# Two mixture-of-experts stages: an earlier weight load on the SP queue, and filler matmuls moved on TensorE

## The chip, the cores and the metric

One core of a Trainium2 chip runs the whole program. The metric is device time in microseconds (us). Before the change it is 985.3 us, the median of three runs (984.91 to 985.96).

## The reference, cut to what matters

The program is one inference step of a two-layer diffusion backbone for 128 context tokens and 256 latent tokens (384 rows of width 1024). Each layer is a mixer followed by a mixture of experts; the change touches only the start of the two mixtures:

```
h = modulate(x, norm2_g, shift, scale)                     # 384 x 1024
p_group, logits_e = softmax(h @ w_group + b), h @ w_expert + b
expert_id, weight = top-1 group, top-2 experts within it   # 768 (token, expert) pairs over 16 experts
hid = silu(h @ w1[e]) * (h @ w3[e])                        # EXPERT_DIM = 256
y   = sum over the two experts of weight * (hid @ w2[e])
x   = x + gate * y
```

## The kernel before, in words

Everything is written out by hand: one program per engine, ordered by semaphores. The mixture stands twice, as `experts(0)` after the attention and recurrence layer and as `experts(1)` after the convolution layer. The 768 pairs are laid into 14 positions of 128 slots (`POSITIONS`); a position serves one or two experts, each with an "up" block (w1 and w3, 2 MB) and a "down" block (w2, 1 MB). The blocks rotate through rings of five buffers (`ring`, `dring`), so the first five up blocks (positions 0, 0, 1, 1, 2) find their buffers empty and the later ones wait for a position to be used.

A mixture begins in this order. The router (VectorE, with small products on TensorE) gives each pair its slot. TensorE turns the normed rows h token-wise (L2139, `h_turned`). ScalarE copies the turned rows out of PSUM (L894, `htok_ready`, six copies) and stores them to `h_rows` in device memory with three DMAs on its own queue (L896, `h_stored`). VectorE builds six comparison columns (L1447, `owners_ready`), TensorE multiplies them (L2145, `owners_T`), and VectorE makes indices of the product (`rows_ready`). GpSimd then waits for `h_stored` and `rows_ready` and picks the rows of positions 0, 1 and 2 from `h_rows` by indirect DMA (L584). TensorE turns the picked rows (`fill`, L2119), ScalarE copies them (`slots`, L882), and the loop over positions begins with `up(0)` (L2094).

Beside that path TensorE has other work before `up(0)`, all in program order: in layer 0 two pairs of products with the last adaLN weights (`ada(2, 6)`, L1694, of which the second pair follows the owners product and needs ScalarE's copy L684 of the pair before), the second owners product with the pairs' weights (L2156, after VectorE's `weights_ready`), and the turned gates (L2158). ScalarE copies the gates (L911), stores them (L915, 4 KB), waits for that store, reads them back broadcast (L918), and only then copies the picked rows of position 0 (L882). `keep(n)` (L1709) issues n matmuls of 128x256 whose result nobody reads; in the trace each is two instructions.

The SP queue carries the weights. Its program is in order too: `static` loads (L445) that wait until a buffer of the adaLN weights is free, `expert_up` (L469) and `expert_down` (L484). In layer 0 the blocks (0,0), (0,1), (1,0) of the down ring lie in buffers of the adaLN weights and wait for `ada_used` 38, the end of the second `ada(2, 6)`; the block (1,1) lies in the buffer of h and waits for `h_turned` and `h_stored`, in both layers; (2,0) has a buffer that is free when the projection before is done.

Of the kernel before, what the change touches and what calls it, by code (L numbers as in the profile page):

```python
# [28 lines left out]
NB = TOK // P  # L29
# [243 lines left out]
def build(nc, A):  # L273
    with ExitStack() as ctx:
        sems = {}

        def S(name):

            if name not in sems:
                sems[name] = ctx.enter_context(nc.semaphore(name))  # L280
            return sems[name]

        def ge(eng, name, v):

            if isinstance(v, int) and v <= 0:
                return
            eng.wait_ge(S(name), v)
# [6 lines left out]
        def bank(b, n=512, o=0):  # L294
            return ps[:, b * 512 + o:b * 512 + o + n]
# [146 lines left out]
        @block.sync  # L442
        def _(sp):
            def load(n, dst, src):
                sp.dma_start(dst, src).then_inc(S(f"raw_full{n % RAW}"), 16)  # L445

            def fetch(n):

                if n < FIRST:
                    sp.dma_start(ada_first(n), A["weights"][n]).then_inc(S(f"ada_full{n}"), 16)  # L450
                else:
                    load(n, raw[:, n % RAW, :], A["weights"][n])

            def static(a, b):
                for n in range(a, b):
                    if n >= FIRST + RAW:
                        name, v = FREED[n - RAW]
                        sp.wait_ge(S(name), v)
                    if B_P1 <= n < B_P1 + RAW:
                        sp.wait_ge(S("down_used"), POSITIONS - 2 if n == B_P1 else POSITIONS)  # L460
                    fetch(n)

            def expert_up(l, q, z):

                m = BLOCK_AT[q, z]
                if m >= RING:
                    sp.wait_ge(S("up_used"), POSITIONS * l + BLOCKS[m - RING][0] + 1)
                e = P * (EXPERTS * l + BLOCKS[m][2])
                sp.dma_start(ring(m).rearrange("p k n -> p (k n)"), A["experts_up"][e:e + P, :]).then_inc(S(f"up_full{m % RING}"), 16)  # L469

            def expert_down(l, q, z):

                m = BLOCK_AT[q, z]
                if m >= RING:
                    sp.wait_ge(S("down_used"), POSITIONS * l + BLOCKS[m - RING][0] + 1)
                elif m == RAW:
                    sp.wait_ge(S("h_turned"), 6 * (l + 1))
                    sp.wait_ge(S("h_stored"), 16 * NB * (l + 1))
                elif l == 0 and m < RAW:
                    sp.wait_ge(S("ada_used"), N_ADA0)  # L480
                else:
                    sp.wait_ge(S("lo_done"), (U_PW1, U_END)[l])
                e = P * (EXPERTS * l + BLOCKS[m][2])
                sp.dma_start(dring(m).rearrange("p k n -> p (k n)"), A["experts_down"][e:e + P, :])\  # L484
                    .then_inc(S(f"down_full{m % RING}"), 16)

            def expert_loads(l):

                for q in range(2):
                    for z in range(2):  # L490
                        expert_up(l, q, z)
                if l == 0:
                    static(B_P1 - 6, B_P1)
                sp.wait_ge(S("unit_used"), (U_PW1, U_END)[l])
                if l == 0:
                    sp.wait_ge(S("h_stored"), 16 * NB)
                    sp.wait_ge(S("picked0"), 16)
                    for q, z in ((0, 0), (0, 1), (1, 0), (1, 1)):
                        expert_down(l, q, z)
                    expert_up(l, 2, 0)  # L500
                    expert_down(l, 2, 0)
                else:
                    expert_up(l, 2, 0)
                    for q, z in ((2, 0), (0, 0), (0, 1), (1, 0), (1, 1)):
                        expert_down(l, q, z)
                expert_up(l, 3, 0)
                for q in range(4, POSITIONS):
                    expert_up(l, q, 0)
                    expert_down(l, q - 1, 0)
                expert_down(l, POSITIONS - 1, 0)  # L510
                if l == 0:
                    static(B_P1, B_P1 + 1)
                for z in range(2):
                    sp.wait_ge(S(f"rows_stored{z}"), 16 * (POSITIONS // 2) * (l + 1))
                for b in range(NB):
                    for c in range(2):
                        sp.dma_start(got[:, c, b, :], y_rows[TOK * c + P * b:TOK * c + P * b + P, :]).then_inc(S(f"got_rows{b}"), 16)
                if l == 0:
                    sp.wait_ge(S("up_used"), POSITIONS)
                    sp.dma_start(inverse, A["shape_constants"][:, T_I:T_I + I_W]).then_inc(S("in_inverse"), 16)  # L520

            static(0, B_P1 - 6)

            sp.wait_ge(S("oblo_ready"), 4)
            sp.wait_ge(S("oalo_ready"), NB)
            sp.wait_ge(S("pv_done"), len(PAIRS))
            expert_loads(0)
            static(B_P1 + 1, len(SLOTS))
            sp.wait_ge(S("cs_ready"), KC)
            expert_loads(1)  # L530

            for b in range(NB):
                sp.wait_ge(S("rows_added"), 2 * NB + b + 1)
                dst = A["out0"][0] if b == 0 else A["out1"][0, P * (b - 1):P * b, :]
                sp.dma_start(dst, got[:, 0, b, :]).then_inc(S("out_y"), 16)
            sp.wait_ge(S("out_kv"), 32)
            sp.wait_ge(S("out_state"), 64)
            sp.wait_ge(S("out_y"), 48)
# [1134 lines left out]
        def _(pe):  # L1673
# [25 lines left out]
            def keep(n, out=None, left=par[:, A_WR:A_WR + P], right=par[:, A_WR:A_WR + 256]):  # L1699

                if out is None:
                    i = slot[0] % 8
                    if i == 0:
                        ge(pe, "mod_ready", slot[0] // 8 + 1 if slot[0] else 0)
                    if i % 2 == 0:
                        pe.wait_ge(S("adarow_ready"), slot[0] // 2)
                    out = bank(7, 256, 256 * (i % 2))
                for _ in range(n):
                    mm(out, left, right, start=True, stop=True)  # L1709
# [348 lines left out]
            def experts(l):  # L2058
# [78 lines left out]
                for b in range(6):  # L2137
                    for k in range(4 * (b % 2), 4 * (b % 2) + 4):
                        last = nc.tensor.transpose(bank(b, P, P * (k % 4)), hfk[:, k, P * (b // 2):P * (b // 2) + P], ident)  # L2139
                    last.then_inc(S("h_turned"), 1)  # L2140
                if l:
                    keep(6, bank(6, 256))
                for i in range(6):
                    pe.wait_ge(S("owners_ready"), 6 * l + i + 1)
                    ins = mm(bank(7, POSITIONS, 64), column[:, i, :], named[:, i, :], start=(i == 0), stop=(i == 5))  # L2145
                ins.then_inc(S("owners_T"), 1)
                pe.wait_ge(S("htok_ready"), 2 * NB * (l + 1))
                if l == 0:
                    ada(2, 6)
                    pe.wait_ge(S("adarow_ready"), 19)  # L2150
# [103 lines left out]
            norm(1)  # L2254
            ada(2)
            experts(0)

# [81 lines left out]
            for j in range(2, 8):  # L2340
# [6 lines left out]
                elif j == 6:  # L2347
                    ada_columns(5)
            norm(3)
            experts(1)  # L2350

# [55 lines left out]
```

## Time and profile before

| | |
|---|---|
| median of three runs | 985.3 us |
| profiled execution: its time | 985.96 us |
| profiled execution: its span | 983.9 us |
| TensorE busy | 900.8 us, 92% of the span |
| VectorE, ScalarE, GpSimd busy | 406.7, 289.7, 263.1 us |
| chain that ended last | TensorE 75%, VectorE 9%, DMA 9%, ScalarE 4% |
| SP's DMA queue (q1) | 189.80 MB, 50.5% of 16 engines' span |

The span is the time of the instructions in the trace; the execution's own time also holds what lies around them. Busy times are averages over stages that differ much: the change is at 366 to 391 us in layer 0 and at 777 to 795 us in layer 1, and is read there.

### The profile page before, as it was taken

The page shows a single profiled execution, that of the slowest core. Times are in us where ns is not written, and L with a number is a line of the kernel's source. Part 1 is how long each engine was busy: PE and PEld are TensorE (multiplying, and loading weights), DVE is VectorE, ACT ScalarE, POOL GpSimd, SP SyncE. Part 2 cuts the span into 40 slices and gives each one's busy share as a digit, 9 for nine tenths or more (in the row PEclk, how much of TensorE's full clock was granted, in tenths as well). Part 3 has the DMA queues.
Part 4 walks back from the last instruction along what each step waited for, and adds up shares of the span by engine and source line. Part 5 has one row for each costly group of instructions (what it writes and reads, how often), then busy time and mean ns, then how long its engine had stood idle before and what let it go on. Part 6 is the DMA issues. An engine that isn't in the chain of part 4 may idle for free.

```text
span 983.9 us, 13906 instructions
## 1 busy us (share of the span) xinstructions
PE 900.8 (92%) x5729; PEld 578.3 (59%) x5729; DVE 406.7 (41%) x762; ACT 289.7 (29%) x537; POOL 263.1 (27%) x175
## 2 busy tenths in 40 slices
PE   3899999978797998998999989999999899989996
PEld 1688898755565985333333379888588743323332
DVE  1653665566635462222223463222625602222245
ACT  2632243332433243111111364121552521101112
POOL 0156353300003301233233306230360113333330
PEclk9999999998996997999999999999999889999998
DMA  9675335412424958999886543330449959999815
GB/s 379 261 257 214 129 135 204 149 44 89 171 91 145 419 177 322 403 378 401 299 313 230 186 163 129 129 130 1 174 179 417 364 187 377 403 362 380 294 64 202
DMA packets 41598, 230.08 MB, mean 234 GB/s; under 512 B 14112, under 2 KB 15168, under 8 KB 21824
## 3 DMA queue, kind: packets, MB, share of 16 engines
q1 hardware_dynamic: 22608, 189.80, 50.5%
q0 software_dynamic: 14528, 28.61, 8.1%
q10 hardware_dynamic: 4400, 10.77, 3.1%
q8 instruction: 46, 0.75, 0.3%
q14 instruction: 16, 0.13, 0.0%
HBM read 279.58 MB, written 19.81 MB: 304 GB/s over the span
## 4 chain that ended last, share of the span: by engine, by line
PE 75%; DVE 9%; DMA 9%; ACT 4%; issue 2%; POOL 1%; ACTq 0%; POOLq 0%; DVEq 0%
PE ps L2094 17%; PE ps L1723 8%; PE ps L2108 8%; PE ps L1725 8%; PE ps L1724 8%; PE ps L1694 4%; DMA Z<-experts_up,par 4%; PE ps L2119 2%; DMA att<-h_rows,par 2%; PE ps L1858 2%; DVE Z L1180 2%; DMA xT<-x_columns 1%; DVE Z L1059 1%; PE ps L1709 1%; PE ps L1715 1%
## 5 line engine op out<-in xcount | busy, mean ns | idle before, releaser
L547 POOL TENSOR_TENSOR wlo<-raw,whi 128x1024 fp32r<-128x1024 f32 x57 | 139.2, 2462 | 355.4 <-ACT whi L663 353.0
L2094 PE MATMUL ps<-Z,att 128*64 128x512 f32 x704 | 192.5, 605 | 6.3 <-DMA Z<-experts_up,par 6.3
L2094 PEld LDWEIGHTS ps<-Z,att 128*64 128x64 f32 x704 | 58.1, 139 | 100.6 <-issue 100.6
L1723 PE MATMUL ps<-hhi,whi 128*128 128x384 f32 x296 | 104.9, 354 | 6.7 <-DVE hlo L1295 3.0
L1724 PE MATMUL ps<-hlo,whi 128*128 128x384 f32 x296 | 101.0, 341 | 0.0
L1725 PE MATMUL ps<-hhi,wlo 128*128 128x384 f32 x296 | 100.9, 341 | 0.0
L1059 DVE TENSOR_TENSOR att<-att,ps 128x256 f32<-128x256 f32 x28 | 11.8, 421 | 190.4 <-ACT att L870 184.7
L663 ACT ACTIVATE whi<-raw 128x1024 fp32r<-128x1024 f32 x58 | 59.8, 1054 | 86.3 <-DMA raw<-weights 56.2
L2108 PE MATMUL ps<-raw,att 128*64 128x512 f32 x272 | 80.2, 598 | 0.0
L1723 PE MATMUL ps<-whi,hhi 128*128 128x256 f32 (+1 forms) x264 | 74.9, 284 | 2.4 <-DVE hlo L1570 1.7
L1724 PE MATMUL ps<-wlo,hhi 128*128 128x256 f32 (+1 forms) x264 | 73.7, 279 | 0.0
L1725 PE MATMUL ps<-whi,hlo 128*128 128x256 f32 (+1 forms) x264 | 73.5, 279 | 0.0
L2094 PE MATMUL ps<-spare,att 128*64 128x512 f32 x160 | 72.4, 595 | 0.0
L597 POOL DMA_INDIRECT y_rows<-att,par x28 | 34.2, 1222 | 138.7 <-DVE att L1507 137.1
L1507 DVE SCALAR_TENSOR_TENSOR att<-ps,par,slot_gate 128x512 f32<-128x512 f32 x52 | 39.0, 750 | 72.5 <-PE ps L2108 72.5
L1723 PEld LDWEIGHTS ps<-hhi,whi 128*128 128x128 f32 x296 | 56.9, 192 | 16.9 <-issue 8.7
L875 ACT ACTIVATE att<-ps 128x256 f32<-128x256 f32 x28 | 10.7, 384 | 169.6 <-PE ps L2076 169.5
L1724 PEld LDWEIGHTS ps<-hlo,whi 128*128 128x128 f32 x296 | 57.0, 193 | 0.0
L1725 PEld LDWEIGHTS ps<-hhi,wlo 128*128 128x128 f32 x296 | 56.7, 192 | 0.0
L1180 DVE COPY_PREDICATED Z<-con,ps 128x1024 f32<-128x1024 uint32 x24 | 31.0, 1311 | 53.6 <-PE ps L1858 36.5
L584 POOL DMA_INDIRECT att<-h_rows,par x28 | 28.3, 1011 | 89.6 <-DVE par L1463 42.2
L1723 PEld LDWEIGHTS ps<-whi,hhi 128*128 128x128 f32 x264 | 49.7, 188 | 4.3 <-issue 3.2
(332 smaller groups left out, 1487.0 us busy)
## 6 DMA issues: line engine op xcount, KB each, us to landing
raw<-weights SPq DMA_DIRECT2D x69, 1024.0 KB, 4.9
Z<-experts_up SPq DMA_DIRECT2D x26, 2048.0 KB, 10.8
raw<-experts_down SPq DMA_DIRECT2D x20, 1024.0 KB, 9.0
spare<-experts_up SPq DMA_DIRECT2D x6, 2048.0 KB, 12.1
Z<-weights SPq DMA_DIRECT2D x8, 1024.0 KB, 16.5
hf<-experts_down SPq DMA_DIRECT2D x6, 1024.0 KB, 9.1
spare<-experts_down SPq DMA_DIRECT2D x6, 1024.0 KB, 8.9
Z<-y_rows SPq DMA_DIRECT2D x12, 512.0 KB, 6.0
```

The costliest lines, as they stand in the source:

```text
L547: nc.gpsimd.tensor_tensor(unit_view(wlo, u), raw_unit(n, half), unit_view(whi, u).bitcast(F32), ALU.subtract)\
L584: pool.indirect_dma_start(picked[q % 3], None, h_rows[:, :], bass.IndirectOffsetOnAxis(ap=ri[:, OVERFLOW + ORDER[q]:OVERFLOW + ORDER[q] + ...
L597: pool.indirect_dma_start(y_rows[:, :], bass.IndirectOffsetOnAxis(ap=ri[:, o:o + 1], axis=0), rows, None, bounds_check=2 * TOK - 1, oob_is ...
L663: nc.scalar.activation(unit_view(whi, u), raw_unit(n, half), ACT.Copy)\
L1180: V.copy_predicated(AT[:, b, :, :], mask[:, l, :].unsqueeze(1).broadcast_to([P, HEADS, P]), bank(gram_bank(i), 1024).rearrange("p (n i) -> ...
L1507: V.scalar_tensor_tensor(out=dst[:, c], in0=bank(4 + d), scalar=slot_weight[:, n:n + 1], in1=slot_gate[:, c], op0=ALU.mult, op1=ALU.mult). ...
L1694: last = mm(ps[q:q + COLS, o:o + 256], scond[:, k, :], weights[:, k, :], start=(k < 4), stop=(k >= 4))
L1723: mm(out, ahi, bhi, start=start, stop=False)
L1724: mm(out, ahi, blo, start=False, stop=False)
L1725: return mm(out, alo, bhi, start=False, stop=stop)
L2094: last = mm(out, h[:, k, c:c + HALF], ring(BLOCK_AT[q, z])[:, k, :], start=(k == 0), stop=(k == KC - 1))
L2108: last = mm(ps[HALF * z:HALF * z + HALF, 512 * (4 + d):512 * (5 + d)], hcol[q % 2][:, k, HALF * z:HALF * z + HALF], dring(BLOCK_AT[q, z])[ ...
```

## The change

In layer 0 the SP queue no longer waits for `h_stored` and `picked0` as such before its first down blocks. It issues the up block (2,0) as soon as the projection before is used up, then the down blocks (2,0), (1,1), (0,0), (0,1), (1,0), each with the wait that `expert_down` has for its buffer. Layer 1 keeps its order.

On TensorE, in both layers, the wait for all six copies of the turned rows moves from behind the first owners product to ahead of it, and fillers stand between the two: 3 in layer 0 (where there were none) and 10 in layer 1 (where there were 6, ahead of the wait). They write bank 4, which the copies read.

```diff
                 sp.wait_ge(S("unit_used"), (U_PW1, U_END)[l])
-                if l == 0:
-                    sp.wait_ge(S("h_stored"), 16 * NB)
-                    sp.wait_ge(S("picked0"), 16)
-                    for q, z in ((0, 0), (0, 1), (1, 0), (1, 1)):
-                        expert_down(l, q, z)
-                    expert_up(l, 2, 0)
-                    expert_down(l, 2, 0)
-                else:
-                    expert_up(l, 2, 0)
-                    for q, z in ((2, 0), (0, 0), (0, 1), (1, 0), (1, 1)):
-                        expert_down(l, q, z)
+                expert_up(l, 2, 0)
+                for q, z in (((2, 0), (1, 1), (0, 0), (0, 1), (1, 0)), ((2, 0), (0, 0), (0, 1), (1, 0), (1, 1)))[l]:
+                    expert_down(l, q, z)
...
                     last.then_inc(S("h_turned"), 1)
-                if l:
-                    keep(6, bank(6, 256))
+                pe.wait_ge(S("htok_ready"), 2 * NB * (l + 1))
+                keep((3, 10)[l], bank(4, 256))
                 for i in range(6):
                     pe.wait_ge(S("owners_ready"), 6 * l + i + 1)
                     ins = mm(bank(7, POSITIONS, 64), column[:, i, :], named[:, i, :], start=(i == 0), stop=(i == 5))
                 ins.then_inc(S("owners_T"), 1)
-                pe.wait_ge(S("htok_ready"), 2 * NB * (l + 1))
                 if l == 0:
                     ada(2, 6)
```

## Rows read from the trace of the kernel before

**Rows 1.** Timeline of TensorE, layer 0: start us, us, line, operation, idle before and releaser.
```profile
355.19 1.93 PE L1694 MATMUL ps<-raw,scond 128*32 128x256 f32 x32
...
370.88 1.51 PE L2145 MATMUL ps<-att 128*128 128x14 f32 x12 [0.96 <-DVE att L1447]
375.12 3.64 PE L1694 MATMUL ps<-raw,scond 128*32 128x256 f32 x32 [2.74 <-issue]
379.47 2.74 PE L2156 MATMUL ps<-att 128*128 128x14 f32 x12 [0.71 <-ACT adarow L684]
...
382.67 5.37 PE L1709 MATMUL ps<-par 128*128 128x256 f32 x14
...
390.92 9.66 PE L2094 MATMUL ps<-Z,att 128*64 128x512 f32 x44
```

**Rows 2.** One stretch: PE, PEld, DVE, ACT, POOL busy, granted clock, DMA share, GB/s.
```profile
373.00:374.00 1.00, 0.00 (x0) 0.00 (x0) 0.92 (x5) 1.00 (x1) 0.00 (x0) 0.63 1.07 422
```

**Rows 3.** Timeline of ScalarE and its queue, layer 0.
```profile
371.89 0.33 ACTq L896 DMA_DIRECT2D h_rows<-att  x1
...
389.18 1.09 ACT L882 ACTIVATE att<-ps 128x512 f32<-128x512 f32 x2 [5.84 <-PE ps L2119]
```

**Rows 4.** Timeline of the SP queue, layer 0.
```profile
319.92 46.74 SPq L445 DMA_DIRECT2D raw<-weights  x6
380.15 1.28 SPq L484 DMA_DIRECT2D raw<-experts_down  x3
```

**Rows 5.** DMA queues from 392 to 399 us: packets, MB, share of 16 engines.
```profile
q1 hardware_dynamic: 153, 1.99, 66.5%
q10 hardware_dynamic: 134, 1.03, 34.9%
```

**Rows 6.** DMA issues at 371.89, 376.71 and 782.60 us: KB, us to landing.
```profile
h_rows<-att ACTq DMA_DIRECT2D x1, 512.0 KB, 4.0
...
att<-h_rows,par POOLq DMA_INDIRECT x1, 3.3
...
att<-h_rows,par POOLq DMA_INDIRECT x1, 5.8
```

**Rows 7.** Timeline of GpSimd: the first pick of each layer.
```profile
376.71 1.10 POOL L584 DMA_INDIRECT att<-h_rows,par  x1 [39.46 <-DMA h_rows<-att]
...
782.60 1.03 POOL L584 DMA_INDIRECT att<-h_rows,par  x1 [42.19 <-DVE par L1463]
```

**Rows 8.** Timeline of TensorE, layer 1.
```profile
776.79 2.76 PE L1709 MATMUL ps<-par 128*128 128x256 f32 x12
779.38 1.41 PE L2145 MATMUL ps<-att 128*128 128x14 f32 x12
...
784.00 1.48 PE L2156 MATMUL ps<-att 128*128 128x14 f32 x12 [0.96 <-DVE par L1476]
...
788.49 1.97 PE L2119 MATMUL ps<-con,att 128*128 128x128 f32 x8 [2.68 <-DMA att<-h_rows,par]
...
794.35 10.52 PE L2094 MATMUL ps<-Z,att 128*64 128x512 f32 x48
```

**Rows 9.** Timeline of ScalarE, layer 1.
```profile
777.04 1.08 ACT L894 ACTIVATE att<-ps 128x512 f32<-128x512 f32 x2 [0.40 <-PE ps L2139]
...
791.36 1.08 ACT L882 ACTIVATE att<-ps 128x512 f32<-128x512 f32 x2 [4.96 <-DMA gate_rows<-gates]
```

**Rows 10.** Timeline of the SP queue, layer 1.
```profile
756.78 0.33 SPq L469 DMA_DIRECT2D spare<-experts_up  x1
...
781.75 0.33 SPq L484 DMA_DIRECT2D hf<-experts_down  x1
```

**Rows 11.** The chain of waits: the load that TensorE waits for in each layer's loop.
```profile
442.28 19.65 DMA Z<-experts_up,par
...
845.71 19.39 DMA Z<-experts_up,par
```

**Rows 12.** Timeline of TensorE where that load has come, layer 0.
```profile
462.18 5.24 PE L2094 MATMUL ps<-Z,att 128*64 128x512 f32 x16 [3.15 <-DMA Z<-experts_up,par]
```

## The prediction

> **What bounds the kernel now.** The page's busy shares and the chain that ended last say TensorE (92% busy, 75% of the chain). An average says little here, so I went on to the timeline of TensorE around the change. In layer 0 [rows 1] the reader is to see the idle gaps 369.92 to 370.88 and 372.39 to 375.12 us (each row gives the gap ahead of it), and that afterwards the same instructions take about twice as long: the adaLN pair 3.64 us against 1.93, the owners product 2.74 against 1.51. The granted clock tells why: it fell from 2.4 to 1.2 GHz at about 373.3 us [rows 2]. The 14 filler instructions took 5.37 us, where fillers at 2.4 GHz cost 0.23 each [rows 8], so it came back only towards 387. From 379.47 us to `up(0)` at 390.92 TensorE has no gap: its own slow program sets the start of the loop. ScalarE's copy of the picked rows, behind the gate store, ends at 390.27 us (389.18 + 1.09) [rows 3], 0.65 us ahead of `up(0)`: nearly as late. The picks have slack: GpSimd issues the first at 376.71, it lands 3.3 us later at 380.0 [rows 6, 7], and TensorE comes to it when its fillers end at 388.0.
>
> In layer 1 [rows 8] the picks do bind: TensorE waits 2.68 us for one that landed at 788.4 (782.60 plus 5.8) [rows 6, 7], and `up(0)` starts at 794.35. ScalarE's copy ends at 792.44 after its wait for the gate store [rows 9]: 1.9 us of slack. From `up(0)` on, both loops run alike. The chain shows the same late load, issued 51.4 us after `up(0)` in both (442.28 less 390.92, 845.71 less 794.35) and 19.65 and 19.39 us long [rows 11]. So what the change is worth is how far the two starts of `up(0)` move.
>
> **SP queue, layer 0.** The queue is busy with adaLN weights until 319.92 + 46.74 = 366.66 us [rows 4], so the up block (2,0), 2 MB, goes out at about 367 and not at the end of the projection, and the down block (2,0), 1 MB, behind it; before, all six blocks began at 380.15 [rows 4]. That the loop's first blocks come earlier saves nothing: no position waited for them. Nor does it spare the late load: layer 1 issued the same blocks long before its picks (756.78 us) [rows 10] and has the same one.
>
> The cost is where these 3 MB now travel: beside the three h stores of 0.5 MB on ScalarE's queue, of which the last is issued at 371.89 and lands 4.0 us later, at 375.9 [rows 3, 6]. The last adaLN weights end at about 371; from there (3 x 1.05 + 3 x 0.52) / 0.43 = 10.9 us give a last store at 381.5. Bounds: 375.9 (no contention), 378 (shares equal by bytes: 1.57 / 0.216 = 7.3 us), and 381.5. I take 380.5, near the row's rule.
>
> GpSimd went on 0.8 us after the last landing (376.71 less 375.9); now at 381.3. The block (1,1) waits for the same stores, and (0,0), (0,1), (1,0) are ready by then, so 4 MB start right with the picks. One 1 MB block in that place made a pick 5.8 us instead of 3.3 [rows 6, 10]. So pick 0 lands at 381.3 + 5.8 = 387.1 and pick 1, issued 1.3 us later and behind more, between 388.5 and 391; I take 390. Behind it come the turning, 1.97 us at 1.2 GHz [rows 8] or half of it at 2.4, and `up(0)`: 391.0 to 392.0.
>
> **TensorE, layer 0.** The copies end when the third store is issued, 371.89 [rows 3]. TensorE is now idle from 369.92 to 371.9, 2.0 us. Then 3 fillers (6 instructions at 0.23) run to 373.3; the clock falls about there, as it did after the idle 1.0 us, 1.5 us of owners and 0.9 idle of before. The owners product ends at 376.0 (2.74 us at 1.2 GHz) instead of 372.39. What waits for it: the indices, which VectorE makes within a microsecond, hidden behind stores that land later; and the adaLN pair, which started at 375.12 before, when a copy of ScalarE's let it. It runs 376.0 to 379.7, 0.9 us later than before, and all up to the gates with it: 383.6 for 382.7. Fillers and turnings shift by as much or, once the clock is back at 387, by half, and end at about 391.4; ScalarE's copy starts 6.5 us behind the gates as before (389.18 less 382.67): 390.1 to 391.2. Two chains so give `up(0)` at 391.4 and at 391 to 392. I take 392.0: +1.1 us. Bounds: 387.2 (rival A) and 394 (last store 381.5, pick 1 10 us after its issue, turning at 1.2 GHz).
>
> Beside the rows: the Trainium skill, "TensorE: Matmul & The Clock Gate", Part 1, says that the activity window of the clock runs free, so that one kernel can meet it at another phase in another run. No run here shows it for these gaps; by it the clock need not fall at 373.3, and the layer would go as in rival A.
>
> **TensorE, layer 1.** The last copy ends at 777.04 + 1.08 = 778.12 [rows 9]; the wait costs 1.2 us of idle after 776.95. Ten fillers are 20 instructions at 0.22 to 0.23 (12 took 2.76, and 2.59 to the start of the next row), 4.5 us: to 782.6. The owners product ends at 784.0 and not at 780.8 [rows 8]: 3.2 us later. Who waits: the indices, so GpSimd picks at about 785.0 (a microsecond behind the product) instead of 782.60. But the block that it collided with, issued at 781.75 [rows 10], is then nearly through; a pick of 3.3 to 4.5 us lands at 788.3 to 789.5, against 788.4. Then the second product, at 784.00 after VectorE before, at 787.2 now; the gates behind it, 3.2 us later; and ScalarE's copy, which waits for their store: 791.36 + 3.2 = 794.55 to 795.65. TensorE, without its 2.68 us of waiting, has turned position 1 (turnings 1.0 each, four fillers 1.8) by 792.7 to 794.4, so `up(0)` follows that copy at 795.65: +1.3 us. If TensorE then stands 3 us, as in [rows 12], its first 16 instructions take 5.24 us there against 3.5 (a third of the 10.52 of 48) [rows 8]: up to +3.0. Bounds 0 (the wait is hidden) and +3.0; I take +1.6, nearer to the plain sum, since fillers slowed by the clock fill that wait.
>
> **Sum.** 1.1 + 1.6 = +2.7 us. The profiled execution goes from 985.96 to 988.7, its span from 983.9 to 986.6. It lies 0.66 us above the median of the runs, so the median goes from 985.3 to 988.0.
>
> **Rivals.** A, the other side: in layer 0 the stores are hardly delayed and the clock stays at 2.4 GHz. Owners product to 374.7, adaLN pair 375.1 to 377.0, second product and gates to 379.6 (1.5 + 0.3), fillers 3.1 us, turnings and two fillers: `up(0)` at 386.6 by TensorE, 387.2 by the gate store (379.6 + 6.5 + 1.1). That is -3.7; with +1.3 to +1.6 in layer 1, 983.2. It decides, as one mechanism (gates ahead of picks), if the last store lands before about 377.5. For it: the blocks start behind weights that end just when the first store goes. Against: [rows 5], and 2.0 us of idle in one piece.
>
> B, the parts cancel: stores share by bytes and land at 378, pick 1 at 387, `up(0)` near 389.6, -1.3 in layer 0, +1.3 in layer 1: 985.3.
>
> C, the fillers of layer 1 run at 1.2 GHz: 1.2 us idle, then 20 instructions at up to 0.45 (5.37 / 14 = 0.38 in a mixed stretch), 3 to 4 us more on owners, picks and gates alike: +6, 991.5. For it: in this layer too a gap cost the clock (the turning of 1.97 behind 2.68 idle) [rows 8]. Against: the owners product behind 0.96 idle took 1.51 us, the price at 2.4 GHz [rows 1].
>
> D, the early blocks do relieve the late load of layer 0 and its stall of 3.15 + 1.7 us goes [rows 12]: 983.2 with the forecast's +2.7. Against it stands layer 1.
>
> **How the numbers follow.** Forecast 45%, A 20%, B 22%, C 10%, D 3%. What a measurement can tell here is 0.2%, 2.0 us. The forecast's own range is 986.5 to 990.5, of which four fifths are slower by over 0.2%; A is faster by over that in three quarters; B splits 3, 16, 3; C is slower, D faster. Faster 0.15 + 0.03 + 0.03 = 0.21, slower 0.36 + 0.10 + 0.03 = 0.49, same 0.30. The range 983.0 to 991.2 leaves out the ends of A and C.
>
> **What would show it.** In the profile after: the third h store of layer 0 takes 8 us or more (right) or about 4 (A); the first pick at 381 and not 377; the clock at 1.2 GHz from 373; `up(0)` at 392 and 796 to 799 (the latter on top of the former's shift); the owners product of layer 1 ends 6 us after the last copy; ScalarE's copy of position 0 there is the last thing before `up(0)`. It is wrong if the stores keep their 4 us, if the loop's late load shrinks, or if `up(0)` of layer 1 comes less than 1 us later than layer 0's shift explains.

## The result and the profile after

| | before | after |
|---|---|---|
| median of the runs made together | 985.1 us (4 runs) | 998.75 us (4 runs) |
| ratio after to before | | 1.0124, 95% interval 1.0102 to 1.0145 |
| profiled execution: time, span | 985.96, 983.9 us | 996.26, 994.2 us |
| TensorE busy | 92% | 90% |
| DMA in the chain that ended last | 9% | 12% |

The changed kernel is slower by 1.2%. The record holds 21 executions of it in all, 994.2 to 1001.4 us with a median of 997.2; the ratio goes with these, while the four alone would give 1.4%. The prediction was 988.0 us, range 983.0 to 991.2: the direction was right, the size was not.

The SP queue in layer 0 after, from the timeline (start us, us, line, what). It answers to [rows 4, 10]:

```profile
366.15 0.43 SPq L469 DMA_DIRECT2D spare<-experts_up  x1
366.62 0.43 SPq L484 DMA_DIRECT2D spare<-experts_down  x1
383.91 0.33 SPq L484 DMA_DIRECT2D hf<-experts_down  x1
384.28 1.63 SPq L484 DMA_DIRECT2D raw<-experts_down  x3
```

The two early blocks go out as soon as the last adaLN weights have, as predicted, and the other four when the h stores have landed: at 383.9 us, not at 376.

The chain of waits after, layer 0: the two DMAs that now stand in it (start us, us), where before only the gate store stood.

```profile
371.32 12.52 DMA h_rows<-att
...
384.72 10.20 DMA att<-h_rows,par
```

The third store, 4.0 us before [rows 6], takes 12.5; the first pick, 3.3 before, takes 10.2. TensorE's timeline after, layer 0, answers to [rows 1]:

```profile
371.35 1.56 PE L1701 MATMUL ps<-par 128*128 128x256 f32 x6 [2.00 <-ACT att L886]
372.75 1.41 PE L2137 MATMUL ps<-att 128*128 128x14 f32 x12
374.31 1.93 PE L1686 MATMUL ps<-raw,scond 128*32 128x256 f32 x32 [0.16 <-ACT adarow L676]
377.37 1.48 PE L2147 MATMUL ps<-att 128*128 128x14 f32 x12 [1.12 <-DVE par L1468]
...
379.10 4.98 PE L1701 MATMUL ps<-par 128*128 128x256 f32 x14
394.96 1.97 PE L2111 MATMUL ps<-con,att 128*128 128x128 f32 x8 [10.88 <-DMA att<-h_rows,par]
396.72 1.91 PE L1701 MATMUL ps<-par 128*128 128x256 f32 x4
398.43 1.91 PE L2111 MATMUL ps<-con,att 128*128 128x128 f32 x8
400.27 10.52 PE L2086 MATMUL ps<-Z,att 128*64 128x512 f32 x48
```

Up to the gates TensorE is earlier than before: in this execution the clock stayed at 2.4 GHz until 379.8 (adaLN pair 1.93 us, second product 1.48), and the gates are done by 379.1. Behind its fillers TensorE stands 10.9 us for the pick and comes back at 1.2 GHz (turning 1.97 and 1.91 us, four filler instructions 1.91). `up(0)` starts at 400.3, not 390.9. Three stretches with the columns of [rows 2] show the granted clock (the third value from the end): full, then half behind the gates, and half again in the long wait.

```profile
376.00:379.00 3.00, 1.88 (x24) 1.52 (x16) 2.18 (x15) 0.60 (x1) 0.00 (x0) 1.00 1.01 376
380.00:383.00 3.00, 3.00 (x9) 2.34 (x8) 0.00 (x0) 0.00 (x0) 0.00 (x0) 0.50 0.99 382
387.00:400.00 13.00, 5.04 (x20) 4.47 (x20) 0.00 (x0) 1.67 (x3) 1.16 (x2) 0.50 0.96 397
```

How the two queues shared, from the DMA view of 371 to 378 us after (queue, packets, MB, share of the 16 engines), as in [rows 5] for another stretch:

```profile
q1 hardware_dynamic: 183, 2.15, 79.6%
q10 hardware_dynamic: 159, 0.59, 20.4%
```

The two queues move packets in nearly equal numbers, so the stores with their 4 KB packets get 0.08 MB per us beside 0.31 for the weights. The Trainium skill, "DMA: Bandwidth & Descriptors", Queues, rings and completion order, says that an engine drains a whole group of some 9 to 17 descriptors from one queue before it turns to the next. In this trace every half microsecond from 371.5 to 380.5 holds packets of both queues, but which engine carried which was not looked at, so how finely one engine alternates is not shown. Either way the stores share the engines with the blocks.

TensorE's timeline after, layer 1, answers to [rows 8]:

```profile
786.26 4.58 PE L1701 MATMUL ps<-par 128*128 128x256 f32 x20 [0.69 <-ACT att L886]
790.68 1.41 PE L2137 MATMUL ps<-att 128*128 128x14 f32 x12
...
798.19 1.10 PE L2111 MATMUL ps<-con,att 128*128 128x128 f32 x8 [1.08 <-DMA att<-h_rows,par]
...
803.12 1.06 PE L2111 MATMUL ps<-con,att 128*128 128x128 f32 x8 [2.10 <-ACT att L874]
804.11 10.52 PE L2086 MATMUL ps<-Z,att 128*64 128x512 f32 x48
```

Here the turning of position 1 waits 2.10 us for ScalarE's copy of position 0, which comes behind the gate store as predicted, and `up(0)` follows that turning.

To compare executions, starts are counted below from the first matmul of the router (32 instructions with `send`, 350.24 us in layer 0 before, 349.68 after; 756.68 and 764.53 in layer 1). `up(0)` then starts at 40.7 and 50.6 us in layer 0 (+9.9), at 37.7 and 39.6 in layer 1 (+1.9). The stretch from `up(0)` of layer 0 to the router of layer 1 is 1.5 us shorter, the rest behind is 0.5 longer, the start 0.6 earlier: +10.3 in all, the difference of the spans.

### The profile page after: what moved, and what is told of

Same layout as the page of the kernel before. It is cut to its first block, busy times and chain, and to the rows that moved or that the text cites. A ratio compares the mean times of both kernels' runs of the same rounds, so it can differ in the third digit from the quotient of the medians.

```text
span 994.2 us, 13932 instructions
## 1 busy us (share of the span) xinstructions
PE 897.4 (90%) x5743; PEld 576.9 (58%) x5743; DVE 407.9 (41%) x762; ACT 290.4 (29%) x537; POOL 263.7 (27%) x175
## 4 chain that ended last, share of the span: by engine, by line
PE 71%; DMA 12%; DVE 9%; ACT 4%; issue 2%; POOL 1%; ACTq 0%; POOLq 0%; DVEq 0%
PE ps L2086 14%; PE ps L1715 9%; PE ps L2100 9%; DMA att<-h_rows,par 8%; PE ps L1717 8%; PE ps L1716 8%; PE ps L1686 4%; PE ps L2111 3%; PE ps L1850 2%; DVE Z L1172 2%; DMA xT<-x_columns 1%; DVE Z L1051 1%; PE ps L1701 1%; DMA h_rows<-att 1%; PE ps L1873 1%
## 5 line engine op out<-in xcount | busy, mean ns | idle before, releaser
L2086 PE MATMUL ps<-Z,att 128*64 128x512 f32 x704 | 189.6, 596 | 5.6 <-DMA Z<-experts_up,par 5.6
```

The costliest lines, as they stand in the source:

```text
L2086: last = mm(out, h[:, k, c:c + HALF], ring(BLOCK_AT[q, z])[:, k, :], start=(k == 0), stop=(k == KC - 1))
```

## The experiments

"Before" is the kernel before, run on the same chip with the experiments of its batch: median 986.7 us over 31 runs in the first batch, 986.6 over 28 in the second, 985.9 over 23 in the third. Its runs lie between 981.4 and 993.5, so differences below 2 us are read from the traces, of which each experiment has one.

**The SP queue's order alone** (`e1_sp_only`): the change without its second hunk.

```diff
-                pe.wait_ge(S("htok_ready"), 2 * NB * (l + 1))
-                keep((3, 10)[l], bank(4, 256))
+                if l:
+                    keep(6, bank(6, 256))
                 for i in range(6):
...
+                pe.wait_ge(S("htok_ready"), 2 * NB * (l + 1))
```

> The SP queue's new order in layer 0, with TensorE's fillers and wait as before. Theory Q (the queue: the early 3 MB delay the three h stores, and the 4 MB released with them delay the picks): nearly all of the +12 us is here, 994 to 998 us; third h store 11 to 13 us instead of 4.0, first pick about 10 us instead of 3.3. Rival F (the fillers and the earlier wait on TensorE carry it): 985 to 987 us.

Measured 995.5 us, ratio to before 1.0081 (1.0049 to 1.0113): +8.8 us. The third store took 11.4 us, the first pick 9.1, and `up(0)` of layer 0 started at 49.5; layer 1 stayed at 37.3. Theory Q holds: the order of loads carries most of the loss. In this trace the second pick bound as well: the second turning waited 1.77 us for it.

**TensorE's hunk alone, and each layer of it alone** (`e2_fill_only`, `e3_fill_l0`, `e4_fill_l1`): the second hunk on the kernel before, in both layers, in layer 0, in layer 1.

```diff
-                if l:
+                if l == 0:                       # e3; l == 1 in e4; always in e2
+                    pe.wait_ge(S("htok_ready"), 2 * NB * (l + 1))
+                    keep((3, 10)[l], bank(4, 256))
+                elif l:
                     keep(6, bank(6, 256))
```

> TensorE's wait and fillers as changed, the SP queue as before. Theory Q: the stores keep 4.0 us and the first pick 3.3; layer 0 starts up(0) 2 to 3.7 us earlier since the clock stays at 2.4 GHz and the gates come at 379 us instead of 382.7; layer 1 starts 1.3 to 2 us later behind ten fillers: 983 to 985 us. Rival F: 990 us or more.

> Only layer 0's wait and 3 fillers are new; SP queue and layer 1 as before. Theory Q: 981.5 to 983.5 us (up(0) of layer 0 2 to 3.7 us earlier, nothing lost in layer 1). Rival F (the fillers hold back the owners product and by it the picks): 985 to 987 us.

> Only layer 1's wait and 10 fillers are new; SP queue and layer 0 as before. As predicted, the owners product of layer 1 comes 3.2 us later and ScalarE's copy behind the gate store sets up(0): 986.4 to 988.1 us. Rival (the wait is hidden, the picks lose no time): 985.1 us, unchanged.

| | median us | ratio, 95% interval | `up(0)` layer 0 | layer 1 |
|---|---|---|---|---|
| both layers | 988.1 | 1.0021 (0.9998 to 1.0044) | 42.0 | 39.9 |
| layer 0 | 985.7 | 0.9983 (0.9961 to 1.0004) | 38.3 | 37.3 |
| layer 1 | 989.9 | 1.0031 (1.0011 to 1.0050) | 41.0 | 39.7 |

`up(0)` of layer 1 starts at 37.3 to 37.7 us in the four traces with the old fillers there and at 39.3 to 39.9 in the eight with ten behind the wait: 2 us, every time. Layer 0's part gave 2.4 us in one trace and cost 1.3 in another, with the same code. The same three instruction groups in these two, first with both layers changed (and the second turning of that trace), then with layer 0 alone:

```profile
372.71 1.71 PE L1709 MATMUL ps<-par 128*128 128x256 f32 x6 [2.00 <-ACT att L894]
374.21 2.58 PE L2145 MATMUL ps<-att 128*128 128x14 f32 x12
376.72 3.64 PE L1694 MATMUL ps<-raw,scond 128*32 128x256 f32 x32
...
391.19 1.94 PE L2119 MATMUL ps<-con,att 128*128 128x128 f32 x8 [3.32 <-ACT att L882]
```

```profile
372.24 1.56 PE L1709 MATMUL ps<-par 128*128 128x256 f32 x6 [2.00 <-ACT att L894]
373.63 1.41 PE L2148 MATMUL ps<-att 128*128 128x14 f32 x12
375.45 1.93 PE L1694 MATMUL ps<-raw,scond 128*32 128x256 f32 x32 [0.41 <-ACT adarow L684]
```

The same 2.00 us gap, and behind it the clock falls to 1.2 GHz at 374.0 in one execution and only at 380.7, behind the gates, in the other. It moves the gates, which are done 31.8 and 29.4 us after the router's start (32.4 before). It is not all of the 1.3 us that the first one lost: its gates were still 0.6 us earlier than before, but their store took 1.1 us longer until ScalarE went on, and the second turning, which waits for ScalarE's copy behind that store, ran at 1.2 GHz (1.94 us for 1.06). Why the store took longer was not tested. My expectations for both layers (983 to 985) and for layer 0 (981.5 to 983.5) counted on the second and were missed; layer 1 alone came out 3.2 us slower by the medians (ratio 1.0031), just above the 1.3 to 3.0 expected of it, with 2.1 of them in the start of its loop.

**How much the store waits, by what is ahead** (`e7_down_early`, `e10_up_early`): of the two early blocks only one goes ahead of the stores, the other waits for `h_stored`.

```diff
-                expert_up(l, 2, 0)
-                for q, z in (((2, 0), (1, 1), (0, 0), (0, 1), (1, 0)), ...)[l]:
+                if l:
+                    expert_up(l, 2, 0)
+                expert_down(l, 2, 0)             # e10: expert_up here, and no down
+                if l == 0:
+                    sp.wait_ge(S("h_stored"), 16 * NB)
+                    expert_up(l, 2, 0)
+                for q, z in (((1, 1), (0, 0), (0, 1), (1, 0)), ...)[l]:
                     expert_down(l, q, z)
```

> The changed kernel, but of the two blocks ahead of the stores in layer 0 only the down block (1 MB in 8 KB packets) goes early; the up block waits for the stores. If a store packet waits for one packet of the other queue each time, the store's landing grows with the time of the packets ahead: 4.0 + 8 x 0.305 = 6.4 us for the third store (4.0 with nothing ahead, 12.5 with both). Rival (two queues at once slow each other whatever is ahead): 9 us or more.

> As the run before it, but only the up block (2 MB in 16 KB packets) goes early and the down blocks wait for the stores. By packets: 4.0 + 8 x 0.61 = 8.9 us for the third store. Rival (a fixed slowing while two queues are busy): the same time as with the down block alone.

The third store's row in each trace (KB, us to landing), down block ahead, then up block ahead:

```profile
h_rows<-att ACTq DMA_DIRECT2D x1, 512.0 KB, 7.2
```

```profile
h_rows<-att ACTq DMA_DIRECT2D x1, 512.0 KB, 9.4
```

With nothing ahead 3.4 to 4.1 us, with 1 MB 7.2, with 2 MB 9.4, with both 11.4 to 12.5: over 4.0 that is +3.2, +5.4, and +7.4 to +8.5 together, near the sum of the two. The wait follows what is ahead, against the rival; the two came out 0.8 and 0.5 us above what was expected from the packets' own time. Each is one execution (991.3 and 995.0 us). The up block has both more bytes and larger rows, so which of the two counts is not told apart.

**What slows the picks** (`e5_downs_behind_pick`, `e6_all_behind_stores`, `e8_gate_row_late`), all on the changed kernel: the four down blocks wait for the first pick again; or every block of the six waits for the stores; or ScalarE's 1 MB gate load goes out behind its copies of the picks.

```diff
                 for q, z in (((2, 0), (1, 1), (0, 0), (0, 1), (1, 0)), ...)[l]:
+                    if l == 0 and (q, z) == (1, 1):          # e5
+                        sp.wait_ge(S("picked0"), 16)
                     expert_down(l, q, z)
...
+                if l == 0:                                   # e6
+                    sp.wait_ge(S("h_stored"), 16 * NB)
                 expert_up(l, 2, 0)
...
-                act.dma_start(gate_row, ...)                 # e8, layer 0
                 slots(0)
                 slots(1)
+                act.dma_start(gate_row, ...)
```

> The changed kernel, but the four down blocks of layer 0 behind the first ones again wait for the first pick to land. Theory Q, with its two costs apart: the stores still take 11 to 13 us beside the early 3 MB, but the first pick, now without 4 MB beside it, lands in 3.5 to 6 us instead of 10.2; up(0) of layer 0 some 5 to 6 us earlier than in the changed kernel: 990 to 993 us. Rival (the delay of the stores is all, the picks are slow for another cause): no gain, 996 us or more.

> The changed kernel, but in layer 0 the SP queue waits for the h stores before it issues anything. Theory Q: the third store takes 4.0 us again; 7 MB now start with the picks, so the first pick takes 8 to 12 us and lands about 36 us after the router's start (45 in the changed kernel, 30 in the kernel before): 985 to 989 us. Rival (the picks' slowness costs more than the stores' in the changed kernel): above 992 us.

> The changed kernel, but in layer 0 ScalarE issues the 1 MB broadcast load of the gates behind its copies of the first two picks and not ahead of them. Theory: that load shares the DMA engines with the picks too; without it the first pick takes 7 to 8.5 us instead of 10.2 and up(0) comes 1.5 to 3 us earlier: 994 to 996 us. Rival (the SP blocks alone slow the picks): unchanged, 997 to 999 us.

| beside the picks | third store us | first pick us | `up(0)` layer 0 | median us (ratio) |
|---|---|---|---|---|
| nothing (before) | 4.0 | 3.3 | 40.7 | |
| gate load (e5) | 12.5 | 5.4 | 45.1 | 991.9 (1.0055) |
| 4 MB of down blocks (e8) | 11.7 | 8.3 | 47.4 | 996.1 (1.0095) |
| both (after) | 12.5 | 10.2 | 50.6 | 997.2, 21 runs (1.0124) |
| 7 MB (e6) | 4.1 | 10.0 | 41.1 | 987.7 (1.0008) |

The pick's time is from its issue to the turning that waits for it. The row of the turning with the down blocks held back shows the shorter wait:

```profile
389.13 1.97 PE L2113 MATMUL ps<-con,att 128*128 128x128 f32 x8 [7.71 <-DMA att<-h_rows,par]
```

The pick grows with what runs beside it. Two more traces fit in: with 5 and 6 MB of blocks behind the stores (e10, e7), and the gate load beside the pick's last 2 us, it took 8.7 and 9.5. With the stores at 4 us again, the slow picks cost nothing against the kernel before (e6): they fall into the slack of 7.9 us that it had there. Its gates, though, came at 29.4, as in e3, whose `up(0)` starts at 38.3. Against that kernel the slow picks cost 2.8 us, of which TensorE's wait for the first was 2.24: they used up what the TensorE part had gained.

```profile
388.53 1.71 PE L2113 MATMUL ps<-con,att 128*128 128x128 f32 x8 [2.24 <-DMA att<-h_rows,par]
```

It is the two delays on end that go past the slack. The rival for e6 falls.

**Ten fillers or the wait, in layer 1** (`e11_l1_three`): layer 1's wait moved as in the change, with 3 fillers.

```diff
-                if l:
+                if l == 1:
+                    pe.wait_ge(S("htok_ready"), 2 * NB * (l + 1))
+                    keep(3, bank(4, 256))
+                elif l:
                     keep(6, bank(6, 256))
```

> The kernel before with layer 1's wait for the copies moved ahead of the owners product, but with 3 fillers behind it instead of 10. Theory: the 2 us of layer 1 are the length of ten fillers; with three the owners product begins 22.8 us after the router's start, as in the kernel before (22.7; 26.1 with ten), and up(0) at 37 to 38: the time of the kernel before within 1 us. Rival (the wait itself costs): up(0) at 39 or later, +2 us.

Measured 985.5 us, ratio 0.9990 (0.9968 to 1.0012). The owners product begins at 22.9, as expected, but `up(0)` at 38.5 instead of 37 to 38: in this trace the third store took 4.4 us and not 3.5, and the first pick landed 1.1 us later for it, without the fillers' doing. The time is that of the kernel before, so the length of the ten fillers, not the wait, is most of what the change pays in layer 1.

**Covering the idle time** (`e9_cover`) and **picks ahead of gates** (`e12_picks_ahead`), built on the kernel before.

```diff
-                if l:
-                    keep(6, bank(6, 256))
+                if l == 0:
+                    pe.wait_ge(S("htok_ready"), 1)
+                keep((4, 6)[l], bank(6 if l else 0, 256))
...
                 pe.wait_ge(S("htok_ready"), 2 * NB * (l + 1))
+                if l == 0:
+                    keep(3, bank(4, 256))
...
-                keep((7, 0)[l], bank(4, 256))        # from here on e12 alone
+                keep((2, 0)[l], bank(4, 256))
                 fill(0)
-                keep((2, 4)[l], bank(4, 256))
+                keep((2, 1)[l], bank(4, 256))
...
+                slots(0)
                 act.wait_ge(S("h_stored"), 16 * NB * (l + 1))
                 act.wait_ge(S("gates_out"), 32 * (l + 1))
                 act.dma_start(gate_row, ...)
-                slots(0)
                 slots(1)
```

> The kernel before with TensorE's idle time in layer 0 covered: 4 fillers in bank 0 ahead of the owners product (behind the first copy), 3 in bank 4 behind it; nothing is moved, layer 1 and the SP queue as before. If the clock is what held layer 0 back (1.2 GHz from 373 to 387 us in the trace before), up(0) comes 2.5 to 3.7 us earlier in every run, 983 us against 986 to 987 of the kernel before on the same chip, and at least as early as with 3 fillers behind the wait (38.3 us after the router's start). Rival (the gates' store or the picks bind anyway): within 1 us of the kernel before.

> The kernel with the idle time of layer 0 covered, and further: in both layers ScalarE copies the first picked rows ahead of its wait for the gate store, and fewer fillers stand between the gates and the picks (2 and 2 instead of 7 and 2 in layer 0, 0 and 1 instead of 0 and 4 in layer 1). If picks and not gates then set the start, up(0) comes at 33 to 35 us in layer 0 (36.6 in that kernel, 40.7 before) and at 35 to 36.5 in layer 1 (37.3): 980 to 982 us where the kernel before has 985 to 987. Rival (the granted clock falls in the gap that the fillers filled, and up(0) itself runs slower): no gain over that kernel.

Covering alone: 985.3 us, 0.9989 (0.9973 to 1.0005). In its trace `up(0)` of layer 0 starts at 36.6, 4.1 us earlier, but the medians show 1.3 us and not the 3 expected, and that not clear of their spread. With the picks ahead: 983.4 us, 0.9967 (0.9948 to 0.9986), 2.5 us faster than the kernel before on its chip by the medians and so faster than both kernels, if less than expected (980 to 982). `up(0)` starts at 34.7 and 35.5, as expected. That is 6.0 and 2.2 us earlier, and the loop gave a part back: from `up(0)` of layer 0 to the router of layer 1 this trace has 369.5 us against 365.8 before, with 7.8 us of waits of TensorE for picks and weights where the kernel before has 4.1. The DMA engines have little room there:

```profile
384.00:470.00 86.00, 81.72 (x360) 31.88 (x361) 17.74 (x22) 13.48 (x27) 21.30 (x20) 0.96 0.99 392
```

This is the kernel before, with a DMA share of 0.99 from 384 to 470 us. TensorE's timeline of the faster kernel, layer 0:

```profile
378.58 1.76 PE L1709 MATMUL ps<-par 128*128 128x256 f32 x4
380.13 1.91 PE L2119 MATMUL ps<-con,att 128*128 128x128 f32 x8
381.84 1.29 PE L1709 MATMUL ps<-par 128*128 128x256 f32 x4
382.96 1.04 PE L2119 MATMUL ps<-con,att 128*128 128x128 f32 x8
383.93 10.52 PE L2094 MATMUL ps<-Z,att 128*64 128x512 f32 x48
```

The first turning still meets 1.2 GHz (1.91 us), but no wait stands before it.

## Why the prediction was wrong, point by point

- **What bounds layer 0.** Right in part for the kernel before. TensorE's own program ran at 1.2 GHz, and covering the gaps moved `up(0)` by 4.1 us. But the chain that ended last goes through the gate store (4.78 us from 383.93): ScalarE's first copy behind it ends at 389.79, the fillers at 389.78, and the second turning needs both. Where TensorE had its gates earlier (e3), it waited 1.17 us for that copy; in the trace of e9 the gates came 3.3 us earlier and their store took 1.7 us less until ScalarE went on.
- **The early blocks delay the stores.** Right as a mechanism, short in size. "10.9 us give a last store at 381.5" (371 and 10.9 are 381.9), and 380.5 taken: measured 383.8, which is 384.4 when the two traces are laid on each other at the router's start. I summed at 0.43 MB per us; beside 4 KB packets the two queues together moved 2.15 + 0.59 MB in 7 us, 0.39 per us, which would have given 383.1. That they "alternate by packet" was read from counts over 7 us, which show equal numbers and not the order.
- **The step that failed: the first pick at "5.8 us instead of 3.3".** I named 4 MB beside it and priced it by a row with one block of 1 MB; and I left out that the gates, done at 379 now, bring their 1 MB load to the same place. Measured 10.2 us; 8.3 without the gate load, 5.4 with it alone. The trace before had a nearer row: layer 0's third pick, issued at 379.46 with the same blocks issued from 380.15 on, took 7.0 us. Of the 8.8 us by which the start of `up(0)` came later than the 392.0 predicted, the pick makes 4.4 and the store 3.9. My bound of "394" did allow 10 us for a pick, but with its own terms (381.5, 0.8, 1.3, 10, 1.97) it should have been 395.6, and its store was 2.9 us early; the start came at 400.8 on that clock.
- **What comes behind the pick.** I took the second pick for the last and counted one turning behind it, up to 1.97 us. The second turning did not wait, so the first pick set the start, and behind it come two turnings and the fillers between, 5.3 us at 1.2 GHz after the long wait (400.27 less 394.96), against 3.0 before. In all: store +8.5, pick +6.9, the end +2.3, less the slack of 7.9 between landing and turning before: +9.8, measured +9.9, predicted +1.1.
- **The clock in layer 0.** I had it fall at 373.3. It stayed up until the gates were done in the profiled execution and in four others with this code (e3, e5, e6, e7), and fell behind the gap in three (e2, e8, e10). That did not set the start in the changed kernel, since picks did; the 1.2 GHz behind the long wait did count, in the line above.
- **Layer 1.** Right in chain and size: +1.9 for +1.6, with ScalarE's copy behind the gate store in the way. But the plain sum was +1.3, with position 1 turned by then. In fact that turning (1.0 us) waits for the copy too and stands between it and `up(0)`; the 0.3 us that I added for fillers slowed by the clock came closer to it by luck, since these four took 1.89 us, the price at 2.4 GHz.
- **The late load in the loop (rival D).** The stretch behind `up(0)` of layer 0 was 1.5 us shorter in the trace after. Over all traces it lies between 364.3 and 369.5 us whichever order the loads had, so a gain there is not shown.
- **Rivals A and B** needed stores that are hardly delayed; e3 shows that A's part on TensorE exists (-2.4 us) when the SP queue leaves it alone, and the clock lets it; it came to 388.6 on the clock of the trace before, not to 387.2. Rival C did not come: the ten fillers of layer 1 took 4.58 us, the price at 2.4 GHz (and its +6 makes 991.3, not 991.5).
- **What stays open.** The spans of the profiled executions differ by 10.3 us, the medians of the four by 13.6, the median of all 21 of the changed kernel and that of the four before by 12.1. The profiled execution after lies 0.93 us below its median and the one before 0.85 above, which is the difference of 10.3 and 12.1. The SP part alone (+8.8) and the TensorE part alone (+1.4) make 10.2, within what their intervals leave open; whether the two together cost more was not tested.

## What to carry to other kernels

Before a weight load is moved earlier, ask which small transfer then runs beside it, and whether somebody waits for that transfer: here loads of 16 and 8 KB rows took four fifths of the DMA engines from a store of 4 KB rows on another queue, and the chain store, gather, compute paid for it twice. Price a transfer under contention by everything that will be in flight, the loads that your own speed-up brings forward included, and not by a row with less beside it; slack is used up by the first delay and the second one comes in full. Fillers belong where the engine would idle anyway; ahead of a product that others wait for, their length is simply added.

## What the runs showed of the hardware that I had not expected

The same 2.00 us gap of TensorE, in the same code, was followed by 1.2 GHz in some executions (owners product 2.58 us) and by 2.4 GHz until past the gates in others (1.41 us). The Trainium skill, "TensorE: Matmul & The Clock Gate", Part 1, says that the activity window runs free and its phase differs between runs; these traces agree in that the same code met both outcomes; the window itself is not in them. The clock moved the gates of layer 0 by 2.3 to 2.5 us: done 29.4 us after the router's start in five traces, 31.7 to 31.9 in three. A change of 2 us in such a place can so be lost in a single execution. The kernel before itself ran between 982.2 and 993.4 us on one chip, and between 981.4 and 993.5 over the three; how much of that is the clock's phase was not measured.
